# Third mixer stage of a hybrid encoder trunk: diagonals on ScalarE, rotation and row sums ahead of the reciprocals, next scores ahead of weighing

## The reference, cut to what matters

```python
def diff_attention(q, k, v, lam, lam_init, subln_g):
    ...
        s = jnp.einsum('bqhmd,bkhmd->bhmqk', q_blk, k).astype(jnp.float32) * scale
        s = jnp.where(mask, s, NEG_INF)
        p = jax.nn.softmax(s, axis=-1)
        att = (p[:, :, 0] - lam * p[:, :, 1]).astype(v.dtype)
        return jnp.einsum('bhqk,bkhe->bqhe', att, v)
```

## Time and profile before

| | us |
|---|---|
| median of 3 runs (3535.18 to 3542.63) | 3538.82 |
| the profiled execution | 3547.76 |
| its span | 3546.0 |

### The profile page before, as it was taken

How to read it: one execution, slowest core, us unless ns; L and a number is a source line. 1 busy time by engine, 2 the same in 40 slices (tenths; PEclk the granted TensorE clock), 3 DMA queues, 4 the chain that set the end, 5 groups by cost and what they waited for, 6 DMA issues and landing times.

```text
span 3546.0 us, 32953 instructions
## 1 busy us (share of the span) xinstructions
PE 2929.2 (83%) x10296; PEld 1865.6 (53%) x10296; DVE 2490.2 (70%) x5295; ACT 832.7 (23%) x2384; POOL 1850.3 (52%) x1508
## 2 busy tenths in 40 slices
PE   8999788798789878886789878888789878877776
PEld 6678444266577534355477534357478434332222
DVE  1411467787887887788887877788897887754445
ACT  2310122322210123322210122322220023322222
POOL 0000044586677534588676634578677744555552
PEclk9989899999899989998889999999799989999999
DMA  4334399999899999999999999999999999999997
GB/s 162 108 95 160 105 416 420 419 367 409 325 379 409 409 412 405 421 408 408 391 395 409 408 394 407 421 371 394 373 359 409 409 417 417 415 422 421 421 421 307
DMA packets 281580, 1295.97 MB, mean 365 GB/s; under 512 B 31808, under 2 KB 32064, under 8 KB 211776
## 3 DMA queue, kind: packets, MB, share of 16 engines
q0 software_dynamic: 216576, 1073.84, 75.2%
q1 hardware_dynamic: 64256, 217.94, 16.4%
q10 hardware_dynamic: 576, 2.10, 0.1%
HBM read 1291.65 MB, written 2.10 MB: 365 GB/s over the span
## 4 chain that ended last, share of the span: by engine, by line
PE 44%; DMA 26%; DVE 13%; POOL 7%; issue 6%; ACT 4%; DVEq 0%; POOLq 0%; SPq 0%; ACTq 0%
PE bank L581 20%; DMA ring<-in_peer,eidx 16%; PE bank L823 11%; DMA work<-in_peer,eidx 9%; POOL ring L1163 6%; PE bank L785 4%; DVE ring L1196 3%; DVE acc L1201 3%; PE bank L656 2%; PE bank L802 2%; PE bank L632 1%; ACT dg L917 1%; DVE work L1196 1%; PE bank L611 1%; PE bank L635 1%
## 5 line engine op out<-in xcount | busy, mean ns | idle before, releaser
L1163 POOL DMA_INDIRECT ring<-in_peer,eidx x808 | 997.8, 1235 | 396.1 <-issue 219.9
L1196 DVE CUSTOM_DVE_ANT_0 ring<-ring,hp 128x1024 f32<-128x1024 f32 x816 | 984.1, 1221 | 308.7 <-DMA ring<-in_peer,eidx 308.4
L823 PE MATMUL bank<-ring,dg 128*128 128x512 f32 x1784 | 836.8, 618 | 260.7 <-ACT dg L917 228.7
L1158 POOL DMA_INDIRECT ring<-in_peer,eidx x390 | 483.5, 1240 | 934.8 <-DVE eidx L1292 437.8
L581 PE MATMUL bank<-xt,panel 128*128 128x256 f32 x4096 | 925.1, 384 | 19.7 <-ACT xt L923 5.6
L581 PEld LDWEIGHTS bank<-xt,panel 128*128 128x128 f32 x4096 | 785.2, 193 | 153.4 <-issue 30.9
L823 PEld LDWEIGHTS bank<-ring,dg 128*128 128x128 f32 x1784 | 336.4, 196 | 734.2 <-issue 694.2
L1201 DVE SCALAR_TENSOR_TENSOR acc<-ring,wgt,acc 128x1024 f32<-128x1024 f32 x326 | 415.9, 1287 | 23.0 <-DMA ring<-in_peer,eidx 21.9
L823 PE MATMUL bank<-work,dg 128*128 128x512 f32 x704 | 328.7, 611 | 110.7 <-ACT dg L917 107.6
L1196 DVE CUSTOM_DVE_ANT_0 work<-work,hp 128x1024 f32<-128x1024 f32 x208 | 252.6, 1222 | 124.3 <-DMA work<-in_peer,eidx 124.1
L1158 POOL DMA_INDIRECT work<-in_peer,eidx x154 | 187.1, 1215 | 236.9 <-PE bank L823 162.2
(11 more groups left out here) (174 smaller groups left out, 2470.0 us busy)
## 6 DMA issues: line engine op xcount, KB each, us to landing
panel<-in_panels SPq DMA_DIRECT2D x368, 512.0 KB, 6.8
ring<-in_peer,eidx POOLq DMA_INDIRECT x1198, 16.3
work<-in_rel_bias SPq DMA_DIRECT2D x16, 512.0 KB, 8.1
work<-in_peer,eidx POOLq DMA_INDIRECT x306, 21.9
gb<-in_ln_g SPq DMA_DIRECT2D x8, 512.0 KB, 8.6
gb<-in_ln_b SPq DMA_DIRECT2D x8, 512.0 KB, 10.9
panel<-in_keys SPq DMA_DIRECT2D x16, 256.0 KB, 6.2
work<-in_x SPq DMA_DIRECT2D x4, 512.0 KB, 4.6
```

The costliest lines, as they stand in the source:

```text
L823: ins = mm(pa[t * 2 + half][:, :], dg[:, i % DIAGS, :], v_row[:, half * 512:(half + 1) * 512], start=(n == group[0]), stop=(n == group[-1]))
L1158: pool.indirect_dma_start(slots(slot, 2), None, t_in["peer"], bass.IndirectOffsetOnAxis(ap=eidx[:, 0, t, c:c + 1], axis=0)).then_inc(row_i ...
L1163: pool.indirect_dma_start(slots(slot, 1), None, one_row, bass.IndirectOffsetOnAxis(ap=eidx[:, which, t, c:c + 1], axis=0)).then_inc(row_in ...
L1196: v.tensor_tensor_reduce(row, row, hp[:, t, :], 1.0, 0.0, ALU.mult, ALU.add, hid[:, t, c:c + 1]).then_inc(used, 1)
```

## The change

Three things change in stage C; stages A, B, G, O and PEER stay as they are.

1. The four diagonal matrices of a pass are made by ACT (`weights_c`, ahead of take_weighed(u)) instead of DVE. DVE keeps the reciprocals (`inverses`), multiplies those of map 1 by minus lambda, and raises a new semaphore `c_inv` once per map, on which ACT waits.
2. On DVE the two row operations at the end of a pass and rope(u+1) come right after maxima(u), and the reciprocals of pass u after them. The row operations stand ahead of rope(u+1), and no longer behind it.
3. On PE scores(u+1) stands ahead of weigh(u). The order is now scores(0), swap(1), scores(1), weigh(0), outputs(0), project_qk(2), swap(2), scores(2), weigh(1), and so on.

```diff
                 for u in range(UNITS):
-                    weigh("C", s, u)
                     if u + 1 < UNITS:
                         scores("C", s, u + 1)
+                    weigh("C", s, u)
                     outputs("C", s, u)
...
+            def weights_c(s, u):
+
+                n = s * UNITS + u
+                for m in range(2):
+                    act.wait_ge(c_inv, n * 2 + m + 1)
+                    for i in (2 * m, 2 * m + 1):
+                        fn(dg[:, u % 2 * 4 + i, :], ident, ACT.Copy, scale=rinv[:, u % 2, i:i + 1]
+                           ).then_inc(dg_done["C"], 1)
+
...
                 for u in range(UNITS):
+                    weights_c(s, u)
                     take_weighed("C", s, u)
...
+            def inverses(s, u):
+
+                n = s * UNITS + u
+                for m in range(2):
+                    part = rinv[:, u % 2, 2 * m:2 * m + 2]
+                    dve.wait_ge(e_done["C"], n * 4 + m * 2 + 2)
+                    ins = v.reciprocal(part, esum[:, u % 2, 2 * m:2 * m + 2])
+                    if m:
+                        ins.then_inc(*own.one())
+                        step()
+                        ins = ts(part, part, small[:, 13:14], None, ALU.mult)
+                    ins.then_inc(c_inv, 1)
...
                     maxima(kind, s, u)
-                    diagonals(kind, s, u)
-                    if kind == "C" and u + 1 < UNITS:
-                        rope(s, u + 1)
+                    if kind == "A":
+                        diagonals(s, u)
                     rows((s, kind, u, 4))
+                    if kind == "C":
+                        if u + 1 < UNITS:
+                            rope(s, u + 1)
+                        inverses(s, u)
```

More of the change, by code:

```diff
@@ L428, in trunk @@
         dg_done = {k: sem(f"dg_done_{k}") for k in "AC"}
+        c_inv = sem("c_inv")
         rope_done = sem("rope_done")
@@ L1445, in maxima, with diagonals @@
                     rows((s, kind, u, i))
-            def diagonals(kind, s, u):
+            def diagonals(s, u):
                 n = s * UNITS + u
                 for m in range(2):
-                    dve.wait_ge(e_done[kind], n * 4 + m * 2 + 2)
+                    dve.wait_ge(e_done["A"], n * 4 + m * 2 + 2)
                     v.reciprocal(rinv[:, u % 2, 2 * m:2 * m + 2], esum[:, u % 2, 2 * m:2 * m + 2]).then_inc(*own.one())
@@ L1453, in diagonals @@
                     for i in (2 * m, 2 * m + 1):
[L1454 to L1459, removed]
+                        ts(dg[:, u % 2 * 4 + i, :], ident, rinv[:, u % 2, i:i + 1], None, ALU.mult
+                           ).then_inc(dg_done["A"], 1)
+            def inverses(s, u):
[9 more added lines that the diff above has]
+                    ins.then_inc(c_inv, 1)
             def attention_stage(kind, s):
```

## The result

The changed kernel takes 3603.15 us (median of 6 runs, 3598.27 to 3606.88), the kernel before 3540.41 us in the same comparison (6 runs). The ratio is 1.0176, 95% interval 1.0164 to 1.0187: about 63 us slower, inside the range given and 12 us above its likeliest value (+51). The profiled execution of the changed kernel took 3602.7 us, its span is 3600.9 us.

What follows compares the result with a forecast made beforehand. PE was taken to bound slab 0, DVE and PE in turns slabs 1 to 3. Full-clock waits 15.8 + pass 0 clock 16.7 + steady-pass clock 18.5 = +51 us on 3538.8, so 3590 us; range 3556 to 3615.

Steps and rivals of the forecast that it cites:

- Part 1, the order on PE: Steady passes at full clock: scores wait for rope, ACT's copy lies uncovered; +1.5 us per pass in slab 0, +1.6 in slab 1.
- Part 2, pass 0: First pass of each slab at full clock: outputs(0) later by 0.85, 2.0, 2.9 and 2.0 us in slabs 0 to 3.
- Part 3, ACT's diagonals: Diagonals made on ACT: +0.35 us in slab 0's last pass, elsewhere nothing, being beside scores of 4 us or more.
- The last pass: Slabs 1 to 3: DVE releases weigh(3), net 0, so pass 2's delay is taken back there.
- everything slow at once: Case left out of the range, +88 us; last passes of slabs 1 and 3 take 20 against 16.6 us, +4 each.
- Part 4, the clock: Lower PE clock over scores and weighing: 16.7 us in pass 0 of slabs 1 to 3, 18.5 in steady passes.
- half of the scores' price: Steady passes: clock falls in the course of scores, so 9.3 us is taken off 27.8, leaving 18.5.
- The clock holds: Rival: idle in steady passes too short to lower the clock; +15.8 to +32.5 us, 3555 to 3571; chance 0.27.
- Swallowed: Rival: transfers' lead in slab 2 and DVE's saving cancel the full-clock loss, clock holds; within 7 us, 3539; chance 0.07.
- Faster, because DVE was the bound: Rival: slabs 1 to 3 gain DVE's saved time and part of its two waits; 12 us faster, 3527; chance 0.06.

Runs made afterwards that it cites:

- e1: Kernel before with only PE's order changed, scores(u+1) ahead of weigh(u); DVE keeps diagonals, then rope, then rows: ratio 1.0183.
- e3: Changed kernel with weigh(u) put back ahead of scores(u+1) on PE; ACT's diagonals and DVE's new order stay: ratio 1.0192.
- e2: Kernel before with ACT's diagonals alone, PE's order as before, DVE doing maxima, reciprocals, rope, rows: ratio 1.0003.
- e5: Changed kernel with spare matmuls on PE ahead of scores(u+1), 3 each, 12 in pass 0 of slabs 1 to 3: ratio 1.0048.
- e7: Kernel before with some DVE row work of stage C's passes 0 and 3 moved behind diagonals and rope, key R's behind the norm's diagonals: ratio 0.9991.
- e6: Kernel before with spare matmuls where PE waits: ahead of scores(0) (26, slabs 1 to 3), weigh(0) and weigh(3): ratio 0.9986.
- e12: Kernel before with the spare matmuls of e6, but 33 ahead of scores(0) in slabs 1 to 3; DVE's diagonals: ratio 0.9983.
- e4: Changed kernel with spare matmuls on PE ahead of scores(u+1), 7 each, 24 in pass 0 of slabs 1 to 3: ratio 1.0096.
- e8: Kernel before with both the spare matmuls of e6 and the later row work of e7: ratio 1.0026.
- e11: Kernel before with ACT's diagonals and spare matmuls ahead of weigh(0), weigh(3) and, 33 in slabs 1 to 3, scores(0): ratio 0.9982.

## Why the prediction was right, and where its sizes were off

**Part 1, the order on PE.** Right. e1 shows that this edit alone brings the whole loss, and e3 that undoing it does not take the loss away while DVE keeps its new order, which the prediction did not see; the waits are 0.74, 1.58 and 0.57 us; the price of a steady pass at full clock is 1.6 to 1.8 us where 1.5 and 1.6 stood.

**Part 2, pass 0.** Right, with its clock term. From the start of scores(0) to outputs(0): slab 0 11.9 to 15.2 us (+3.3; 0.85 and 2.5 of clock forecast), slab 1 26.2 to 34.6 (+8.4; 2.0 + 6.5), slab 2 20.2 to 26.6 (+6.4; 2.9 + 3.7), slab 3 26.3 to 34.6 (+8.3; 8.5).

**Part 3, ACT's diagonals.** Free, as said (e2). **The last pass** is the term that failed. I let pass 2's delay be taken back in slabs 1 to 3, since weigh(3) was DVE's there, and named 4 us each for slabs 1 and 3 only as what everything slow at once would cost. From outputs(1) to the gate products slab 1 grew by 5.6 us, slab 3 by 5.5, slab 2 by 1.6: 12.7 us. In slab 1 weigh(3) no longer waits for row work, but for the exponentials:

```profile
1010.72 0.59 ACT L954 ACTIVATE ex<-bank,nmax 128x384 f32<-128x384 f32 x1
...
1014.07 0.70 ACT L954 ACTIVATE ex<-bank,nmax 128x512 f32<-128x512 f32 x1
...
1014.74 1.32 ACT L964 ACTIVATE dg<-cst,rinv 128x128 f32<-128x128 f32 x4
...
1014.90 0.17 DVE L1474 RECIPROCAL rinv<-esum 128x2 f32<-128x2 f32 x1 [2.64 <-ACT ex L954]
...
1016.20 6.31 PE L657 MATMUL bank<-dg,ex 128*128 128x128 f32 x28 [3.50 <-ACT dg L964]
```

ACT does pass 3's exponentials only after it has copied the weighed tiles of pass 2, and with slow scores and a slow weigh(2) that is 15 us after scores(3) began (995.54). The prediction let these exponentials lie beside the projection of 7.2 us, at no cost; but in the last pass there is no projection behind the outputs that could cover them. Weigh(3) comes after 20.7 us, where the sum had DVE release it after 16.6 (its row work did end after 16.3, at 1011.88) and my bound said 20; and it takes 6.31 us where it took 4.88. With the clock held up (e5) weigh(3) comes after 16.9 us, and from outputs(1) to the gate products it is 38.7, 32.8 and 37.3 us in slabs 1 to 3, 1.7 us more than before in all. So nearly all of the 12.7 us are the clock's.

**Part 4, the clock.** Right in kind, 47 us by e5 against 35 forecast (16.7 + 18.5). Of the 12 us between, two pieces are the steady passes': I took half of the scores' price there, but in slabs 1 and 3 the scores were slow from their first matmul, +8.0 us for pass 1 instead of 5.9 (4.3 us in both); in slab 0 the clock fell in their course, and two steady passes cost 2.9 and 2.6 us instead of 4.0 each. The rest of the difference is the last pass, which is slow for the clock too (11 of its 12.7 us, by e5).

Together: 51 + 12.7 (last passes) + 4.3 (scores of slabs 1 and 3) - 2.3 (slab 0) = 65.7, and stage C grew by 65.5.

**The rivals.** *The clock holds* is what e5 made true, but for slab 2, and it gave +15 us where +15.8 stood, the last digits by luck (see e5). *Swallowed* fails on the transfers: in the longer stage they idle more (0.76 against 0.88 in slab 1, 0.89 against 0.99 in slab 2) and the time behind the stages shrank by 1.0, 2.3 and 1.3 us only. *Faster, because DVE was the bound* fails on e2, where DVE's saving alone is worth nothing, and on e7, which cut the two waits of slab 1 on its diagonals to 0.82 and 3.15 us and was no faster. What the Trainium skill says (TensorE: Matmul & The Clock Gate, Part 1), that activity releases the clock, again did not hold for the scores: 10 us of them without a pause at 0.50 in four places of slab 1 alone. The advice of the Trainium skill against pauses of PE (the same page, "HAM oscillation — how this bites in real kernels") is borne out by e6 and e5, though standing 1.58 us behind 0.74 us and a swap was enough here.

What stays open: why the clock fell at once in slabs 1 and 3, and later within the scores in slab 0, and why the same instructions of slab 0 kept it in e12 and lost it in e6. The places of fall were not tried one by one.

## What to carry to other kernels

In an in-order list of TensorE, look at what an instruction covers before moving it: weigh(1) looked movable and was the cover of the rotation, and scores the cover of a copy. Then price the clock with the wait: here some 16 us of waits brought some 47 us by the lower clock, and a few spare matmuls in the wait tell the two apart in one run, if they are counted for that wait: e4 and e8 lost by too many. A stage made shorter by postponing work that frees buffers gains nothing where the transfers that need these buffers are the next bound.

## What the runs showed of the hardware that was not expected

Scores(0), matmuls on 64 rows, did not bring the clock back in any kernel where they began at the lower level: 10.1 us in slab 1 and 6.7 us in slab 2 at 0.50. Weighing on 128 rows behind them did in slab 1 within its 5.4 us (granted 0.59). The shorter weighing of slab 2 (2.9 us) ran at the lower level itself; the scores behind it were at full clock in the kernel before, took another 6.7 us at the lower level in e2, and got the clock back after their first tile in e7 (4.4 us). Where the clock was full when they began (958.16 before, e5), the scores of slab 1 kept it for all of their 5.4 us.

Standing 3.45 us ahead of them, after 11.4 us of spare matmuls at full clock, was enough to lose it (e6); 1.04 us (e11) and 0.63 us (e12) let it fall in their course, and 0.58 us kept it (e11). 0.58 and 0.63 us are so close that the length of the last pause can hardly decide alone; what else does, these runs do not show.
